# Rebuilding the state-space stage of a fused two-block kernel: scale folded into the regrouping, spins by pairs, read-out by quarters

## The chip, the cores and the metric

The kernel runs on one core of a Trainium2 chip. The metric is the device time of one execution in microseconds (us), lower is better. The core's engines are TensorE (PE in the rows; PEld is its weight load), VectorE (DVE), ScalarE (ACT), GpSimd (POOL) and SyncE (SP), which here only issues DMAs. Every matmul, transpose, vector and scalar operation is written by hand in the order in which its engine executes it, and semaphores tie the engines together.

## What is computed

Two blocks of a model with 256 tokens and width 1024, one after the other, all in fp32: pooling mixer, stick-breaking attention, two softmax attentions, an MLP, a state-space mixer (S5) with a gated linear unit, and another MLP. The change is in the S5 mixer:

```python
def s5_mixer(h, ...):                       # h = rms_norm(x) * gain, 256 x 1024
    u = h.reshape(S, 64 groups, 16)
    bu = einsum('gpi,lgi->lgp', b_bar, u)   # complex, 64 states per group
    hs = scan(h_t = a_bar * h_{t-1} + bu_t) # along the 256 tokens
    y = einsum('gop,lgp->lgo', c, hs).real + d_skip * u
    g = gelu(y)
    val, gate = split(g @ w_glu, 2)
    return val * sigmoid(gate)
```

## The kernel before

**The S5 stage.** The 256 tokens are taken as 32 steps of L = 8 tokens. Inside a step the recurrence is a fixed 128 x 128 matrix per group, the taps; between the steps runs a scan of 32 elements per state. In order:

1. The last products of the first MLP fill four banks (`acc`). VectorE adds each to `x` (line 2151), and for each of the four there is a pair of DMAs, one from SP (line 602) and one from ScalarE (line 1494), that copies `x` into `xch`, with a step's eight tokens side by side. Beside that ScalarE squares `x` (1496), GpSimd makes the root (2218), and VectorE spreads the row scale over a table (`rrow`, 2164). TensorE turns this table into `rmap` (1085), the scale of every step and token.
2. VectorE waits for all eight copies and regroups `xch` into `xg` in four plain copies (2169). TensorE turns `xg` in four units of four transposes (1092), and VectorE empties each turn into `ug` while it multiplies by `rmap` (2177).
3. TensorE makes the drive of the states in four banks, `inject` 0 to 3, of 32 small matmuls each (1105), then the tap product in four banks of 16 matmuls (1117). Its weights are read from a scratch tensor in DRAM by 16 DMAs of SP, `toep_in` (568): part 0, eight of them, before the copies of `x`, part 1, the other eight, after them. They land in the slots of split weights (`whi`, `wlo`) that the weights `val` 0 need next.
4. VectorE runs `spin(n)`, n = 0 to 3, one for each inject bank: it turns the drive by cosines and sines (1667, 1668, 1670, 1671), scans (1674, twice), turns back (1677, 1678) and writes `states` (1682, twice). Most steps wait for the one before them.
5. TensorE adds the states to the tap product, the read-out (1133): banks 0 and 1 (part 0) after spin 1, banks 2 and 3 (part 1) after spin 3. Half 0 of the groups is in banks 0 and 2, half 1 in banks 1 and 3.
6. ScalarE empties the four banks into `yc` (1504), TensorE turns `yc` (1142), ScalarE applies Gelu (1509) and makes the high part `hT_hi` (1514), VectorE the low part (2188), and TensorE begins the product `val` 0 (688 to 690).

**What sets the order of the rest.** A weight is split into a high part by ScalarE (1220, 128x2048, "fill") and a low part by VectorE (1585) for fp32 accuracy from three fast matmuls. The fills of `val` 0, halves 0 and 1, stand on ScalarE ahead of the four emptyings of item 6, and on VectorE behind spin 3. The rows of `val` 0 come by two DMAs of SP (608) that wait for inject 3. SP has one queue, in this order: taps part 0, copies of `x`, taps part 1, read-out weights of part 1 (642), `val` 0, then ring loads.

```python
b = filled(("inject", n))[:, :].rearrange("p (m r c) -> p r m c", m=2, r=2)
link(dve.tensor_tensor(spun, b, both[0], ALU.mult))          # link: wait for its end
dve.tensor_tensor(crossed, b[:, ::-1], both[1], ALU.mult)
for r in range(2):
    ins = dve.tensor_tensor_scan(faded[:, r], fade, driven[:, r], 0.0, ALU.mult, ALU.add)
```

## Time and profile before

| | |
|---|---|
| time, median of 3 runs | 887.88 us (885.32 to 888.23) |
| the profiled execution, its own time | 886.7 us |
| its span in the trace | 884.9 us |
| granted TensorE clock, mean over the span | 0.986 of full speed |
| TensorE busy | 857.9 us, 97% of the span |
| VectorE busy | 592.9 us, 67% |
| ScalarE busy | 440.4 us, 50% |
| DMA, mean | 176 GB/s |

### The profile page before, as it was taken

The numbers are of one execution on the slowest core, as the hardware profiler recorded it, in microseconds if no ns is written. First come the engines' busy times: TensorE is split into PE (matmuls) and PEld (weight loads), VectorE is DVE, ScalarE is ACT, GpSimd is POOL, SyncE is SP. The second block draws the span as 40 slices with busy tenths as digits, with TensorE's granted clock in tenths as the row PEclk, the third lists the DMA queues.
The fourth block names the chain that finished last, engine by engine and source line by source line (L and its number), as shares of the span: only waits on it lengthen the run. The fifth ranks groups of instructions, "written<-read, shape, count | busy, mean of one in ns | idle before, by whom it ended". The sixth has DMA issues, their size and how long they took to land.

```text
span 884.9 us, 13373 instructions
## 1 busy us (share of the span) xinstructions
PE 857.9 (97%) x5611; PEld 744.5 (84%) x5611; DVE 592.9 (67%) x746; ACT 440.4 (50%) x585; POOL 113.1 (13%) x74
## 2 busy tenths in 40 slices
PE   6999999999999999999999999996989999999998
PEld 5886888888788878888999888885978899999996
DVE  4694577766756769787878888773875665555553
ACT  5644465656954656644534436442074544444441
POOL 1000001111000023131333334430000000000000
PEclk9999999999999999999999999998599999999999
DMA  8936645555014438126466556647766555555521
GB/s 294 341 127 232 240 146 191 190 190 182 10 40 149 140 96 285 49 96 214 144 222 202 175 196 217 216 167 156 256 221 207 174 190 191 190 190 190 190 96 48
DMA packets 67253, 155.96 MB, mean 176 GB/s; under 512 B 3017, under 2 KB 6826, under 8 KB 66938
## 3 DMA queue, kind: packets, MB, share of 16 engines
q1 hardware_dynamic: 63888, 146.28, 49.2%
q0 software_dynamic: 2224, 7.67, 2.6%
q10 hardware_dynamic: 1082, 1.16, 0.7%
q8 instruction: 45, 0.74, 0.3%
q14 instruction: 14, 0.11, 0.0%
HBM read 146.70 MB, written 7.34 MB: 174 GB/s over the span
## 4 chain that ended last, share of the span: by engine, by line
PE 88%; DVE 8%; ACT 2%; DMA 1%; issue 1%; ACTq 0%; DVEq 0%
PE bank L688 18%; PE bank L689 18%; PE bank L690 18%; PE bank L1000 7%; PE bank L1002 7%; PE bank L998 7%; PE bank L681 2%; PE bank L783 2%; PE bank L773 1%; DMA work<-x 1%; PE bank L1063 1%; PE bank L884 1%; DVE aux L1674 1%; DMA cst<-in_tables 1%; PE bank L823 1%
## 5 line engine op out<-in xcount | busy, mean ns | idle before, releaser
L1585 DVE TENSOR_TENSOR wlo<-ring,whi 128x2048 fp32r<-128x2048 f32 (+1 forms) x104 | 253.7, 2443 | 139.6 <-ACT whi L1220 139.3
L1220 ACT ACTIVATE whi<-ring 128x2048 fp32r<-128x2048 f32 (+1 forms) x105 | 200.5, 1909 | 214.8 <-PE bank L690 148.3
L688 PE MATMUL bank<-whi,hT 128*128 128x512 f32 (+1 forms) x512 | 201.8, 394 | 4.3 <-DVE hT L2188 2.3
L690 PE MATMUL bank<-whi,hT 128*128 128x512 f32 (+1 forms) x512 | 199.5, 390 | 0.0
L689 PE MATMUL bank<-wlo,hT 128*128 128x512 f32 (+1 forms) x512 | 199.4, 389 | 0.0
L998 PE MATMUL bank<-hT,whi 128*128 128x256 f32 x512 | 145.4, 284 | 0.0
L1000 PE MATMUL bank<-hT,whi 128*128 128x256 f32 x512 | 144.8, 283 | 0.0
L1002 PE MATMUL bank<-hT,wlo 128*128 128x256 f32 x512 | 144.8, 283 | 0.0
L688 PEld LDWEIGHTS bank<-whi,hT 128*128 128x128 f32 x512 | 96.7, 189 | 25.3 <-issue 4.4
L690 PEld LDWEIGHTS bank<-whi,hT 128*128 128x128 f32 x512 | 96.5, 189 | 19.6
L689 PEld LDWEIGHTS bank<-wlo,hT 128*128 128x128 f32 x512 | 96.7, 189 | 19.0 <-issue 0.2
L998 PEld LDWEIGHTS bank<-hT,whi 128*128 128x128 f32 x512 | 98.1, 192 | 0.6
L1000 PEld LDWEIGHTS bank<-hT,whi 128*128 128x128 f32 x512 | 98.2, 192 | 0.5
L1002 PEld LDWEIGHTS bank<-hT,wlo 128*128 128x128 f32 x512 | 98.1, 192 | 0.0
L688 PE MATMUL bank<-whi,hidT_hi 128*128 128x512 f32 x224 | 88.2, 394 | 0.0
L689 PE MATMUL bank<-wlo,hidT_hi 128*128 128x512 f32 x224 | 87.5, 390 | 0.0
L690 PE MATMUL bank<-whi,hidT_lo 128*128 128x512 f32 x224 | 87.2, 389 | 0.0
L1580 DVE SCALAR_TENSOR_TENSOR wlo<-ring,vcols,whi 128x512 fp32r<-128x512 f32 x64 | 43.8, 747 | 20.5 <-ACT whi L1216 20.5
L1216 ACT ACTIVATE whi<-ring,vcols 128x512 fp32r<-128x512 f32 x64 | 40.9, 711 | 19.2 <-PE bank L690 17.0
L688 PEld LDWEIGHTS bank<-whi,hidT_hi 128*128 128x128 f32 x224 | 42.1, 188 | 9.9 <-issue 1.4
L690 PEld LDWEIGHTS bank<-whi,hidT_lo 128*128 128x128 f32 x224 | 42.1, 188 | 8.9
L689 PEld LDWEIGHTS bank<-wlo,hidT_hi 128*128 128x128 f32 x224 | 42.1, 188 | 8.3
(278 smaller groups left out, 1026.9 us busy)
## 6 DMA issues: line engine op xcount, KB each, us to landing
ring<-in_w_ff SPq DMA_DIRECT2D x64, 1024.0 KB, 5.3
ring<-in_ple_gate_w SPq DMA_DIRECT2D x8, 1024.0 KB, 5.1
ring<-in_w_kv SPq DMA_DIRECT2D x8, 1024.0 KB, 5.0
ring<-in_b_w_in SPq DMA_DIRECT2D x8, 1024.0 KB, 5.0
ring<-in_a_w_in SPq DMA_DIRECT2D x7, 1024.0 KB, 13.0
ring<-in_w_in SPq DMA_DIRECT2D x6, 1024.0 KB, 5.3
ring<-in_w_glu SPq DMA_DIRECT2D x6, 1024.0 KB, 6.6
ring<-in_a_w_out SPq DMA_DIRECT2D x4, 1024.0 KB, 5.8
```

Of the source, the lines that this page charges most:

```text
L681: last = pe.transpose(b[0:width, cc * S + t * P:cc * S + t * P + P], src[:, t, c * width:(c + 1) * width], ident)
L688: pe.matmul(bank_cols, high[:, at[0], at[1]], w_high, start=first, stop=False)
L689: pe.matmul(bank_cols, high[:, at[0], at[1]], w_low, start=False, stop=False)
L690: return pe.matmul(bank_cols, low[:, at[0], at[1]], w_high, start=False, stop=last)
L783: last = pe.matmul(b[:, :], pT[:, l, k, t * P:(t + 1) * P], ple_rows[:, k, nb * 512:(nb + 1) * 512], start=(k == 0), stop=(k == 1))
L998: pe.matmul(b[:, at:at + S], w_high[:, kk, cols], hT_hi[:, k, :], start=k == 0 and at == 0, stop=False, skip_group_check=True)
L1000: pe.matmul(b[:, at:at + S], w_high[:, kk, cols], hT_lo[:, k, :], start=False, stop=False, skip_group_check=True)
L1002: last = pe.matmul(b[:, at:at + S], w_low[:, kk, cols], hT_hi[:, k, :], start=False, stop=k == KC - 1, skip_group_check=True)
L1216: ins = act.activation(whi[at][:, n], ring[:, slot[name], cols][:, n], ACT.Copy, scale=gain(gained[name[0]], 4 * (g % 2) + kk))
L1220: act.activation(whi[at], raw_rows(g), ACT.Copy).then_inc(high_made, 1)
L1580: ins = dve.scalar_tensor_tensor(out=wlo[at][:, n], in0=ring[:, slot[name], cols][:, n], scalar=gain(gained[name[0]], 4 * (g % 2) + kk), i ...
L1585: dve.tensor_tensor(wlo[at], raw_rows(g), whi[at], ALU.subtract).then_inc(low_made, 1)
```

## The change

- **Scale.** The table is smaller (`row_of`, 8 columns), `rmap` comes from two accumulated matmuls with the constant `chunk_of`, and VectorE copies it before it waits for the copies of `x`. The four regrouping instructions become multiplications by `rmap`. `xg` lies in another place (over `hT`).
- **Turns.** ScalarE, not VectorE, empties the four turns into `ug`, by plain copies.
- **Taps.** SP issues only the first four of the eight DMAs of part 0 before the copies of `x`, the other four after them, ahead of part 1.
- **Spins.** `spin_pair` takes two inject banks: sums, scans and (for pair 0) the turning back work on both. Pair 1 turns back in two halves and signals after each.
- **Order on TensorE.** Taps part 0, read-out part 0, taps part 1, read-out part 1. The tap product goes through the four output quarters in its inner loop. Read-out part 1 is split in two by quarters of the output, each for both halves of the groups.
- **Emptying.** VectorE empties bank 2, ScalarE banks 0, 1 and 3. ScalarE's fill of `val` 0 half 0 stands between bank 1 and bank 3, its fill of half 1 behind the first two Gelus, and VectorE's low parts are moved to match.
- **Constant matmuls.** `constant_products` puts 14, 4, 8 and 8 fp32 matmuls on a constant into idle banks; nothing reads them.

```diff
+KEEP = (14, 4, 8, 8)
...
     for b in range(4):
-        u.add(("ug", b), "v")
+        u.add(("ug", b), "a")
...
+            u.add(("state_out", n), "v" if n == 2 else "a", bank=n)
...
                 if name == ("readout", 1):
-                    toep_in(0)
+                    toep_in(0, (0,))
...
                     sp.wait_ge(x_chunked, 16 * 8)
+                    toep_in(0, (1,))
                     toep_in(1)
...
+            def constant_products(name, count):
+                idle = begin(name)
+                for _ in range(count):
+                    pe.matmul(idle[:, 0:P], allneg[:, :], allneg[:, :], start=True, stop=True, skip_group_check=True)
+            constant_products(("ug", 0), KEEP[0])
             b = begin(("rmap", 0))
...
+            constant_products(("ug", 0), KEEP[1])
...
-                for q in range(4):
-                    for s in range(4):
+                for s in range(4):
+                    for q in range(4):
                         last = pe.matmul(b[32 * q:32 * q + 32, s * P:(s + 1) * P]...,
...
+            for part in range(2):
+                pe.wait_ge(toep_landed[part], 16 * 8)
+                for half in range(GH):
+                    tap_product(2 * part + half)
+                constant_products(("state_outT", 0), KEEP[2 + part])
+                weights_here(("readout", part))
+                if part == 0:
+                    pe.wait_ge(states_ready, 1)
+                    for half in range(GH):
+                        read_out(0, (half,), range(4))
+                else:
+                    pe.wait_ge(states_ready, 2)
+                    read_out(1, (0, 1), (0, 1))
+                    pe.wait_ge(states_ready, 3)
+                    read_out(1, (0, 1), (2, 3))
...
-            refill(("f2", 0, FB - 2), 1)
-            refill(("f2", 0, FB - 1), 0)
             for n in range(4):
+                b = filled(("ug", n))
+                act.activation(to, b[:, :]..., ACT.Copy).then_inc(act_emptied, 1)
+            for n in (0, 1, 3):
+                if n == 3:
+                    refill(("f2", 0, FB - 2), 1)
                 b = filled(("state_out", n))
...
+            def spin_pair(pair):
+                for odd in range(2):
+                    b = filled(("inject", 2 * pair + odd))...
+                    dve.tensor_tensor(spun[:, :, m], b, both[0][:, :, m], ALU.mult)
+                    dve.tensor_tensor(crossed[:, :, m], b[:, ::-1], both[1][:, :, m], ALU.mult).then_inc(dve_emptied, 1)
...
+                for m in (slice(0, 2), slice(2, 4)) if pair else (slice(0, 4),):
+                    dve.tensor_tensor(spun[:, :, m], faded[:, :, m], both[0][:, :, m], ALU.mult)
+                    link(dve.tensor_tensor(crossed[:, :, m], faded[:, ::-1, m], both[1][:, :, m], ALU.mult))
...
+            b = filled(("rmap", 0))
+            dve.tensor_copy(rmap, b[:, 0:L]).then_inc(dve_emptied, 1)
             dve.wait_ge(x_chunked, 16 * 8)
             for n in range(4):
-                dve.tensor_copy(xg[:, l:l + 4], xch...).then_inc(regrouped, 1)
+                dve.tensor_tensor(xg[:, l:l + 4], xch..., rmap..., ALU.mult).then_inc(regrouped, 1)
```

VectorE from the waiting for the copies of `x` to the first spin. Before (2169 regroups, 2172 copies `rmap`, 2177 empties the turns, from 1667 on the first spin):

```order
L2169 COPY aux<-work 128x512 [waits x_chunked]
L2169 COPY aux<-work 128x512 x3
L2172 COPY aux<-bank 128x32 [waits pe_done]
L2177 TENSOR_TENSOR work<-bank,aux 128x4x4x32 [waits pe_done,dve_emptied]
L2177 TENSOR_TENSOR work<-bank,aux 128x4x4x32 [waits pe_done] x3
L1667 TENSOR_TENSOR aux<-bank,h 128x512 [waits pe_done,fades_ready,waves_ready]
```

And now, with the whole of pair 0:

```order
L2212 COPY aux<-bank 128x8 [waits pe_done]
L2217 TENSOR_TENSOR xg_at<-work,aux 128x512 [waits x_chunked,dve_emptied]
L2217 TENSOR_TENSOR xg_at<-work,aux 128x512 x3
L1710 TENSOR_TENSOR aux<-bank,h 128x2x256 [waits pe_done,fades_ready,waves_ready]
L1711 TENSOR_TENSOR aux<-bank,h 128x2x256
L1710 TENSOR_TENSOR aux<-bank,h 128x2x256 [waits pe_done]
L1711 TENSOR_TENSOR aux<-bank,h 128x2x256
L1713 TENSOR_TENSOR aux<-aux 128x512 [waits dve_emptied]
L1714 TENSOR_TENSOR aux<-aux 128x512
L1717 SCALAR_TENSOR_TENSOR pT<-sig,aux 128x512 [waits dve_step]
...
L1721 TENSOR_TENSOR aux<-pT,h 128x1024 [waits dve_step]
...
L1727 TENSOR_TENSOR aux<-aux 128x4x4x31 [waits dve_step]
```

The copy of `rmap` moved ahead of the wait for the copies of `x`, the emptying of the turns left VectorE, and in pair 0 two instructions stand where four stood for sums and turning back (1717, 1721 and 1727 each come with a second one of the same shape).

SP around the copies of `x`, before (568 taps, 602 copies, 642 read-out weights, 608 `val` 0):

```order
L568 DMA spare<-scratch_taps 128x1x512 x7
L602 DMA work<-x 16x8x256 [waits dve_emptied,pe_done]
L602 DMA work<-x 16x8x256 [waits dve_emptied] x3
L568 DMA spare<-scratch_taps 128x1x512 [waits taps_stored0,zeros_stored,taps_stored1,first_used,x_chunked]
...
L642 DMA ring<-scratch_readout 128x4096 [waits readout_stored1,readout_stored0,low_made]
L608 DMA work<-in_w_glu 128x4x512 [waits pe_done]
```

And now (573, 607, 648 and 614 are the same four):

```order
L573 DMA spare<-scratch_taps 128x1x512 x3
L607 DMA work<-x 16x8x256 [waits dve_emptied,pe_done]
L607 DMA work<-x 16x8x256 [waits dve_emptied] x3
L573 DMA spare<-scratch_taps 128x1x512 [waits taps_stored0,zeros_stored,taps_stored1,f2_done,x_chunked]
...
L573 DMA spare<-scratch_taps 128x1x512 [waits taps_stored0,taps_stored1,zeros_stored,first_used]
...
L648 DMA ring<-scratch_readout 128x4096 [waits readout_stored1,readout_stored0,low_made]
L614 DMA work<-in_w_glu 128x4x512 [waits pe_done]
```

Four transfers of 256 KB went from ahead of the copies to behind them, so that twelve, not eight, stand between the copies and the read-out weights.

## Rows read from the trace of the kernel before

**Rows 1.** The profile's chain that ended last: share of each engine
```profile
PE 88%; DVE 8%; ACT 2%; DMA 1%; issue 1%; ACTq 0%; DVEq 0%
```
**Rows 2.** Busy by stretch: stretch, us, PE, PEld, DVE, ACT, POOL busy, PEclk, DMA share, GB/s
```profile
610.30:614.10 3.80, 0.00 (x1) 0.00 (x0) 1.20 (x5) 2.35 (x3) 0.72 (x1) 1.00 1.05 121
614.10:618.60 4.50, 1.01 (x5) 0.94 (x5) 0.85 (x4) 0.08 (x1) 0.00 (x0) 0.50 0.23 28
618.60:622.20 3.60, 3.60 (x16) 3.27 (x16) 3.51 (x7) 0.00 (x0) 0.00 (x0) 0.50 0.81 214
622.20:636.00 13.80, 13.80 (x257) 13.74 (x256) 10.37 (x19) 0.00 (x0) 0.00 (x0) 0.50 0.77 251
636.00:644.90 8.90, 8.90 (x133) 8.40 (x132) 8.56 (x17) 1.91 (x1) 0.00 (x0) 0.89 0.67 238
...
652.00:656.10 4.10, 1.83 (x16) 1.60 (x17) 1.91 (x3) 4.07 (x6) 0.00 (x0) 1.00 1.05 396
656.10:667.00 10.90, 10.87 (x48) 9.03 (x49) 6.36 (x5) 6.61 (x6) 0.00 (x0) 1.00 0.67 236
```
**Rows 3.** The chain of waits, 590 to 700 us: start, us, what
```profile
611.12 6.80 DMA work<-x
...
622.27 3.58 PE bank L1105 x64
...
648.62 3.35 PE bank L1133 x128
```
**Rows 4.** Timeline, 596 to 700 us: start, us, engine, line, operation; spin 3
```profile
642.95 0.69 DVE L1667 TENSOR_TENSOR aux<-bank,h 128x512 f32<-128x512 f32 x1
643.68 0.69 DVE L1668 TENSOR_TENSOR aux<-bank,h 128x512 f32<-128x512 f32 x1
644.40 0.42 DVE L1670 TENSOR_TENSOR aux<-aux 128x256 f32<-128x256 f32 x1
644.74 0.42 DVE L1671 TENSOR_TENSOR aux<-aux 128x256 f32<-128x256 f32 x1
...
645.19 1.27 DVE L1674 TENSOR_TENSOR_SCAN aux<-sig,aux 128x256 f32<-128x256 f32 x2
646.50 0.69 DVE L1677 TENSOR_TENSOR aux<-aux,h 128x512 f32<-128x512 f32 x1
...
647.11 0.68 DVE L1678 TENSOR_TENSOR aux<-aux,h 128x512 f32<-128x512 f32 x1
647.83 0.74 DVE L1682 TENSOR_TENSOR aux<-aux 128x248 f32<-128x248 f32 x2
```
**Rows 5.** The same timeline, from the last read-out to the product `val` 0
```profile
651.87 1.97 PE L1142 MATMUL bank<-cst,work 128*128 128x128 f32 x16
652.00 0.60 ACT L1504 ACTIVATE work<-bank 128x512 f32<-128x512 f32 x1 [0.76 <-PE bank L1133]
652.56 2.03 ACT L1509 ACTIVATE work<-bank 128x512 f32<-128x512 f32 x2
654.62 1.15 ACT L1514 ACTIVATE hT<-work 128x512 fp32r<-128x512 f32 x2
655.29 1.29 DVE L2188 TENSOR_TENSOR hT<-work,hT 128x512 fp32r<-128x512 f32 x2 [2.19 <-ACT hT L1514]
```
**Rows 6.** DMA issues, 595 to 665 us: queue, count, KB each, median us to landing
```profile
spare<-scratch_taps SPq DMA_DIRECT2D x16, 256.0 KB, 5.1
ring<-scratch_readout SPq DMA_DIRECT2D x1, 2048.0 KB, 11.5
...
work<-x ACTq DMA_DIRECT2D x4, 128.0 KB, 7.0
```
**Rows 7.** Instructions of line 1769: count, duration ns min/median/max
```profile
L1769 DVE TENSOR_TENSOR work<-pa,bb x8: 1211/1213/1219, 432.6 to 594.9; 128x1024 f32<-128x1024 f32 x8
```
**Rows 8.** Groups by line and form, TensorE: count, busy us, mean ns
```profile
L836 PE MATMUL bank<-aux,allneg 128*128 128x128 f32 x32 | 6.5, 286 | 0.0
```
**Rows 9.** The page's groups by line: count, busy us, mean ns, idle before
```profile
L1220 ACT ACTIVATE whi<-ring 128x2048 fp32r<-128x2048 f32 (+1 forms) x105 | 200.5, 1909 | 214.8 <-PE bank L690 148.3
```

More of the change, by code:

```diff
@@ L77, in constants @@
     put("skip_at", i[:, None] % 32 == i[None, :])
[L78 removed]
+    put("row_of", i[:, None] % L == L - 1 - i[None, 0:L])
     put("ramp", np.arange(NC)[None, :])
[L80 removed]
+    put("chunk_of", np.concatenate([(i[None, :] // 16 % NT == t) & (i[:, None] // L == i[None, :] % 16)
+                                    for t in range(NT)], axis=1))
     put("mask_st", np.where(i[:, None] >= i[None, :], BIG, 0))
@@ L222, in plan @@
     for b in range(4):
-        u.add(("ug", b), "v")
+        u.add(("ug", b), "a")
     for b in range(4):
         u.add(("inject", b), "v")
-    for n in range(4):
-        u.add(("toep", n), "", bank=n)
-    for n in range(4):
-        u.add(("state_out", n), "a", bank=n)
+    for part in range(2):
+        for n in (2 * part, 2 * part + 1):
+            u.add(("toep", n), "", bank=n)
+        for n in (2 * part, 2 * part + 1):
+            u.add(("state_out", n), "v" if n == 2 else "a", bank=n)
     for b in range(4):
@@ L555, in _, with toep_in @@
         def _(sp):
-            def toep_in(part):
+            def toep_in(part, pairs=(0, 1)):
                 if part == 0:
@@ L563, in toep_in @@
                     sp.wait_ge(taps_stored[b], 16 * (part + 1))
-                for pair in range(2):
+                for pair in pairs:
                     for s in range(4):
@@ L1084, in _ @@
             for t in range(NT):
-                last = pe.matmul(b[:, 16 * t:16 * t + 16], const("same_j"), rrow[:, t, :], start=True, stop=True)
+                at = slice(P * t, P * t + P)
+                last = pe.matmul(b[:, 0:L], const("chunk_of")[:, at], rrow[:, t, :], start=t == 0, stop=t == NT - 1)
             last.then_inc(pe_done, 1)
+            constant_products(("ug", 0), KEEP[1])
             for n in range(4):
@@ L1120, in _, with read_out @@
                 last.then_inc(pe_done, 1)
-            for n in range(4):
-                b = bank(("state_out", n))
-                part, half = n // 2, n % 2
-                pe.wait_ge(states_ready, 2 * part + 2)
-                rows = slice(GP * half, GP * half + GP)
-                weights_here(("readout", part))
+            def read_out(part, halves, quarters):
                 wr = weights(("readout", part), 32, P)
@@ L1130, in _, with state_turn @@
                     for r in range(2):
-                        for q in range(4):
-                            m = 4 * part + q
-                            last = pe.matmul(b[32 * q:32 * q + 32, s * P:(s + 1) * P],
-                                             states[rows, 8 * m + 4 * r + s, :], wr[rows, 8 * q + 4 * r + s, :],
-                                             start=False, stop=(r == 1), skip_group_check=True)
-                last.then_inc(pe_done, 1)
-            for n in range(4):
+                        for half in halves:
+                            rows = slice(GP * half, GP * half + GP)
+                            for q in quarters:
+                                last = pe.matmul(bank(("state_out", 2 * part + half))[32 * q:32 * q + 32, s * P:(s + 1) * P],
+                                                 states[rows, 8 * (4 * part + q) + 4 * r + s, :], wr[rows, 8 * q + 4 * r + s, :],
+                                                 start=False, stop=(r == 1), skip_group_check=True)
+                            if s == 3 and r == 1 and q == 3:
+                                last.then_inc(pe_done, 1)
+            def state_turn(n):
                 b = begin(("state_outT", n))
                 half = n // 2
-                emptied(("state_out", 2 + half))
+                for part in range(2):
+                    emptied(("state_out", 2 * part + half))
                 for jj in range(4):
@@ L1143, in _ @@
                 last.then_inc(pe_done, 1)
+            for part in range(2):
+                pe.wait_ge(toep_landed[part], 16 * 8)
[12 more added lines that the diff above has]
+                    read_out(1, (0, 1), (2, 3))
+            for n in range(4):
+                state_turn(n)
             for hh in range(2):
@@ L1676, in spin @@
                 link(ins)
[L1677 to L1684 removed]
+                for m in (slice(0, 2), slice(2, 4)) if pair else (slice(0, 4),):
+                    dve.tensor_tensor(spun[:, :, m], faded[:, :, m], both[0][:, :, m], ALU.mult)
+                    link(dve.tensor_tensor(crossed[:, :, m], faded[:, ::-1, m], both[1][:, :, m], ALU.mult))
+                    for r, op in enumerate((ALU.subtract, ALU.add)):
+                        one, two = (v[:, r, m].rearrange("p m (q c) -> p m q c", c=NC)[:, :, :, 0:NC - 1]
+                                    for v in (spun, crossed))
+                        to = states[:, 32 * pair:32 * pair + 32, :].rearrange("p (m r q) c -> p r m q c", m=4, r=2)[:, r, m, :, 1:NC]
+                        ins = dve.tensor_tensor(to, one, two, op)
+                    ins.then_inc(states_ready, 1)
+                    dve.wait_ge(states_ready, (2 if m.start == 0 else 3) if pair else 1)
             def s5_powers():
```

75 lines of the change are left out of this document (33 added, 42 removed).

## The prediction

> **What bounds the kernel now.** I read the chain of the whole execution first: 88% of it is TensorE [rows 1]. So an edit counts only where TensorE waits, or runs slowly while something waits for it. The busy time by stretch shows where [rows 2]: from 610.3 to 656.1 us TensorE is either empty or full of short instructions, and from 656.1 on it is full again (10.87 of 10.90 us) and stays so. I call the start of the product `val` 0, at 656.1, the point P. What comes after P is bound by TensorE and unchanged, so the gain is the time by which P comes earlier.
>
> The chain of waits between the two ends has five links:
> - the last copy of `x`, 6.8 us from 611.1 to 617.9 [rows 3];
> - regrouping and turns, 617.95 to 622.2 = 4.25 us;
> - inject 0 up to spin 0, 3.8 us, of which 3.58 are its matmuls [rows 3];
> - four spins on VectorE, 626.0 to 648.6 = 22.6 us. The steps of one spin [rows 4] begin 0.73, 0.72, 0.34, 0.45, 1.31 (both scans), 0.61 and 0.72 us apart, and the last takes 0.78 up to the next: 5.66 us;
> - the tail, 648.6 to 656.1 = 7.5 us: read-out of two banks 3.35 [rows 3], then 4.1 for emptying, turn, Gelu, high part, low part [rows 5].
>
> The reader should see in rows 2 that the granted clock is 0.50 (1.2 GHz) from 614.1 to 636.0. It fell after TensorE had run nothing from 610.3 to 614.1 (0.00 us busy).
>
> **The change, link by link.**
>
> *Copies of `x`: 1.5 us gained.* Four transfers of 256 KB leave the stretch ahead of the copies, in which the DMA share is full (1.05 in the last piece, [rows 2]). Issue to landing was 7.0 us in the median on ScalarE's queue, and 6.8 for the last. The taps, twice as large per transfer, land in 5.1 us [rows 6]. I put the last copy between these, nearer to the taps because its queue should now be empty: 5.3 us, at 616.4. Bounds: nothing gained (6.8), or 2.3 us (4.5, somewhat under the taps' median, the copies being half as large). The copy of `rmap` must now be done by then; its table is ready at 614.4, and 1 us later it is. It costs nothing under the copies.
>
> *Regrouping and turns: 1.2 us.* Four plain copies become four multiplications of 128x512, which begin 0.61 us apart (line 1677 to 1678, [rows 4]): the last ends at 618.9. A turn of four transposes is 0.9 us at 1.2 GHz (3.6 us for 16, [rows 2]) and 0.5 us at 2.4 GHz (1.97 for 16, [rows 5]), so inject 0 begins at 619.4: 3.0 us instead of 4.25. The turns are emptied by ScalarE, 0.60 us each [rows 5]; it is idle there, and the first inject needs only the second turn. If ScalarE were not idle, the third would still be hidden by inject 0.
>
> *Inject 0: 1.8 us,* all from the clock. At 1.2 GHz 128 matmuls took 13.8 us [rows 2]; at 2.4 GHz I take half, 1.75 us for 32 with 0.25 for handing over. No row shows this shape at 2.4 GHz; the bounds are half and no gain at all. I take half, because transposes halved (3.6 to 1.97). Spin 0 begins at 621.4.
>
> The clock is what the constants are for. A transpose is one record and a fp32 matmul two, so one constant costs about 2 x 1.97/16 = 0.25 us; the row of the same form gives at most 6.5/16 = 0.41 [rows 8]. Fourteen last 3.5 us, from 610.3 to 613.8, just before the table (614.4); at 0.41 they would end at 616.0 and still be hidden by the copies. Four more fill 614.9 to 615.9. The longest idle stretch left is 1.5 us, against the 3.8 that preceded the fall.
>
> *Spins: 1.7 us.* Pair 0: four products of 512, 3 x 0.61 + 0.72 = 2.55; a wait of 0.5 for inject 1, which ends 1.75 us after inject 0 while VectorE is ready after 1.2; sums 0.61 + 0.72 = 1.33; two scans of 512, less than twice 1.31: 2.4; two products of 1024 at 1.2 [rows 7], 2.35; two writes 1.3: together 10.4. Pair 1: 2.55 + 1.33 + 2.4 and twice (0.61 + 0.72 + 0.78): 10.5. Together 20.9 instead of 22.6. Bounds: scans of 2.2 to 2.7 us, so 1.1 to 2.1 gained. The second half of pair 1 is signalled at 621.4 + 20.9 = 642.3, the first at 640.2.
>
> *Tail: 0.85 us.* After the last signal half of a part's read-out is left, 3.35/2 = 1.7 us. Banks 2 and 3 are emptied side by side (0.7), which the first turn (0.5) then waits for; in the old order that turn was hidden behind an emptying. From the first Gelu to P it is 656.1 - 652.6 = 3.5 [rows 5]. With 0.2 for handing over 6.65 instead of 7.5. P is at 649.0.
>
> *What rests on cover.* Tap product, 16 constants and read-out part 0 run under the spins. Injects end at 626.5. In rows 2 the 64 matmuls of the tap product took 8.9 us at a mean clock of 0.89, so at most 4 us a part; taps 0 ends at 630.5, constants 632.5, read-out 0 (spin pair 0 ready at 631.8) 635.9, taps 1 639.9, constants 641.9, then the two quarters-pairs of 1.7: 645.3 instead of 644.0. So with taps as slow as now TensorE is late by 1.3 us. But four consecutive matmuls now write different quarters, as the read-out does, whose 64 matmuls take 3.35 us [rows 3], 1.7 a part; I take this, and nothing is late. The Trainium skill says the same ("TensorE: Matmul & The Clock Gate", section "Part 3: Packing small matmuls — row/col tiling"): matmuls whose outputs lie in different groups of 32 partitions run side by side. By it the sum stands at 7.0; by the row of the tap product it would be 5.7.
>
> The fill of `val` 0 half 0 (1.9 us on ScalarE, [rows 9]) now stands ahead of the emptying of bank 3, so it must start by 642.0. Its rows come behind 3.15 MB of taps and 2.1 MB of read-out weights, 6.3 MB with its own half. At 251 GB/s, the mean of the stretch that held such transfers [rows 2], that is 25 us from 616.4: 641.5. At rest these queues reach 396 GB/s, so it should be nearer 639. I cost it at nothing, with a cover of 0.5 to 3 us. The fill of half 1 (1.9 us) delays the later Gelus; their channels are needed 5.5 us after P (half of the 10.9 for this product, [rows 2]), at 654.5, and are ready about then (649.0 - 0.8 + 1.9 + 2.15 + 1.3 = 653.6).
>
> **The sum.** 1.5 + 1.2 + 1.8 + 1.7 + 0.85 = 7.05 us. Against the profiled execution that is 886.7 - 7.05 = 879.65. The median of the runs is 1.2 above it and gives 887.88 - 7.05 = 880.8. I take the middle, 880.2.
>
> **The rivals.**
>
> *The clock falls all the same.* Then inject 0 takes 3.8, pair 0 waits for inject 1 (3.45 us after inject 0, so 2.2 instead of 0.5), turns end 0.45 later: last signal 642.3 + 0.45 + 1.8 + 1.7 = 646.2. But TensorE is then the later one: injects end 619.9 + 13.8 = 633.7, taps 0 4.0, constants 2.0, read-out 3.35, taps 1 and constants 3.7, read-out 3.35, so 650.1, and P 650.1 + 4.9 = 655.0. A gain of 1.1: 886.2. For it: 13.8 us of injects and 3.6 us of transposes did not lift the clock [rows 2], so perhaps neither holds it. Against it: from 652.0 to 656.1 TensorE ran 1.83 us of transposes and nothing else, and the clock stayed 1.00. The same page of the Trainium skill, "Part 4: PE-mode transpose", states that a transpose does not count as busy in the way a matmul does; by it the stretch from the last constant to inject 0, 615.9 to 619.4, would be 3.5 us of rest, near the 3.8 that was followed by a fall. The turns at 0.50 agree with it, the last stretch does not. Chance 0.15.
>
> *The quarters do not run side by side, or the copies land no earlier.* 5.7 or 5.55 us gained, 881.5 to 882. Within the forecast's own range; chance 0.15. Both together: 883.
>
> *Slower: the weights of `val` 0 come late.* ScalarE waits for them with bank 3, the last turn's source, queued behind. Every us after 642.0 costs one. The gain is gone when the first half lands at 649, that is when 6.3 MB move at under 194 GB/s. At 175 GB/s they land at 652.4, the forecast's P moves by 10.4, and the time is 890.6. For it: the stretches with small transfers had 121 and 214 GB/s [rows 2]. Against it: those held the copies of `x`, or began before the taps flowed; the stretch with taps and read-out weights had 251. Chance 0.06.
>
> **How the numbers follow.** Forecast 0.64, its variants 0.15, clock 0.15, late weights 0.06. A difference of 0.3% (2.7 us, about what a measurement of this kernel can tell from no change) puts the border of faster at 885.2. Forecast and variants lie below it (0.79), of the clock case a fifth (0.03). No change: the rest of the clock case and mild lateness, 0.12. Slower: 0.06. The forecast's own range is 877.5 (copies 0.8 better, scans 0.4, weaker waits) to 883; to hold 8 in 10 with the clock case half in it the range is 877.5 to 886.0.
>
> **What would show it.** Clock 1.00 from 610 through the injects; first regrouping at about 616.4 and not 617.9; inject group 1.75 us, not 3.45; two pairs in 20.9 us; 64 matmuls of taps in 3.5 us; ScalarE's fill of `val` 0 over before bank 3 is full; P at about 649. Wrong it is if the clock drops between 611 and 625, if ScalarE waits for a DMA in front of bank 3, or if TensorE runs constants while a signalled state waits.

## The result, and the profile after

| | median (range), runs | ratio to before, 95% interval |
|---|---|---|
| before | 885.55 us (882.86 to 888.23), 20 | |
| the change | 887.52 us (885.15 to 891.64), 20 | 1.0025 [1.0016, 1.0035] |

The change is 2.0 us slower, where the forecast had 7 us faster. The profiled execution of the change took 885.15 us, the fastest of its twenty; its span is 883.3 us, its mean granted clock 0.996. P is at 654.58 us, not at 649.0. From P to the start of the last matmul, which is what "to the end" means from here on, both kernels take 224.52 us. So the stretch up to P decides, as the prediction assumed.

The busy time by stretch of the change, with the columns of [rows 2]. The stretches are: early constants after the last sum of the MLP, turns, injects, the rest of the spins, taps 1 to read-out 1, tail.

```profile
609.90:613.70 3.80, 3.10 (x28) 2.91 (x27) 1.23 (x5) 2.38 (x3) 0.73 (x1) 1.00 0.56 90
...
616.10:619.80 3.70, 3.67 (x18) 2.78 (x18) 2.84 (x3) 1.79 (x3) 0.00 (x0) 0.55 0.96 249
619.80:630.30 10.50, 8.02 (x257) 7.91 (x256) 7.75 (x10) 0.60 (x1) 0.00 (x0) 0.97 1.08 284
630.30:642.90 12.60, 10.02 (x240) 8.72 (x242) 12.28 (x19) 1.19 (x3) 0.00 (x0) 0.89 0.72 278
642.90:649.40 6.50, 6.48 (x192) 5.89 (x181) 0.00 (x0) 1.81 (x2) 0.00 (x0) 1.00 0.89 305
649.40:654.60 5.20, 1.96 (x17) 1.79 (x17) 3.75 (x4) 4.17 (x6) 0.00 (x0) 1.00 0.79 263
```

The clock did most of what was wanted: it was 1.00 or near it but for two dips to 0.50, of 3.4 us each, from 616.0 (the turns) and from 629.6. The first is one of the forecast's signs of being wrong ("if the clock drops between 611 and 625"), but it cost little: from the start of the regrouping to inject 0 it is 4.72 us, against 4.52 in the second look below, where the clock was 1.00. But in the row of the injects TensorE is busy for 8.02 us of 10.50 with nothing to wait for, and from 642.90 on VectorE stands still (0.00) while TensorE works for 6.5 us. The chain of waits gives both causes; its columns are start, us, what.

```profile
610.70 4.25 DMA work<-x
...
619.83 5.71 PE bank L1120 x190
625.55 2.48 issue
628.02 2.54 PE bank L1120 x66
630.57 3.10 PE bank L1132 x61
633.67 1.20 issue
634.87 0.41 PE bank L1132 x3
635.28 1.98 PE bank L1092 x16
637.26 2.79 PE bank L1145 x109
640.05 1.38 issue
641.43 0.84 PE bank L1145 x19
642.27 1.88 PE bank L1132 x64
644.16 1.98 PE bank L1092 x16
646.14 3.31 PE bank L1145 x128
```

(1120 injects, 1132 taps, 1092 constants, 1145 read-out.) From inject 0 to the end of the read-out the chain never leaves TensorE; in [rows 3] the read-out of the last banks stood behind the spins. And three times, for 5.06 us in all, TensorE stops for nothing that this chain shows. The timeline of the change says how early the states were ready:

```profile
621.97 0.69 DVE L1710 TENSOR_TENSOR aux<-bank,h 128x512 f32<-128x512 f32 x1 [3.02 <-PE bank L1120]
...
642.11 0.75 DVE L1727 TENSOR_TENSOR aux<-aux 128x248 f32<-128x248 f32 x2
...
642.80 1.90 ACT L1254 ACTIVATE whi<-work 128x2048 fp32r<-128x2048 f32 x1
...
649.49 0.69 DVE L2225 COPY work<-bank 128x512 f32<-128x512 f32 x1 [6.63 <-PE bank L1145]
```

Two pairs of spins take 621.97 to 642.86 = 20.9 us, as forecast, and then VectorE waits 6.63 us for the read-out. The gain of the spins exists and reaches nobody. The fill of `val` 0 (line 1254) starts without waiting for a DMA.

### The profile page after: what moved, and what is told of

It is laid out like the page before. It is cut to its first block, busy times and chain, and to the rows that moved or that the text cites. A ratio compares the mean times of both kernels' runs of the same rounds, so it can differ in the third digit from the quotient of the medians.

```text
span 883.3 us, 13493 instructions
## 1 busy us (share of the span) xinstructions
PE 856.6 (97%) x5679; PEld 741.8 (84%) x5679; DVE 590.8 (67%) x731; ACT 442.1 (50%) x588; POOL 113.0 (13%) x74
## 4 chain that ended last, share of the span: by engine, by line
PE 87%; DVE 5%; DMA 3%; ACT 2%; issue 1%; SPq 1%; ACTq 0%; DVEq 0%
PE bank L694 18%; PE bank L696 17%; PE bank L695 17%; PE bank L1008 7%; PE bank L1006 7%; PE bank L1004 7%; PE bank L687 2%; DMA ring<-in_a_w_in 2%; PE bank L789 2%; PE bank L1120 1%; DMA x<-in_x 1%; PE bank L1145 1%; PE bank L779 1%; DVE wlo L1625 1%; PE bank L1069 1%
```

## What the kernel before does in another execution

The prediction rested on one execution of before (886.7 us, 1.1 above the median now known). **A second look at before**, unchanged:

> The kernel before, unchanged, for a second profile. Its runs have mean granted clocks of 0.986 to 0.994, and the profile that the prediction used had 0.986. Theory: that profile showed one of the rarer executions, with 23.9 us at half clock; in most the clock comes back after one piece of a few us, and the injects run at full clock already. Then this profile, if its clock is about 0.993, shows injects in 7 to 10 us instead of 13.8 and the product val 0 begins some 2 to 4 us earlier after the last sum. If its clock is 0.986 again it says nothing new.

Measured: 883.7 us. The injects and the tail in its busy time by stretch, then TensorE's rows of its timeline:

```profile
620.10:631.20 11.10, 9.22 (x257) 9.11 (x256) 8.56 (x16) 0.00 (x0) 0.00 (x0) 0.81 0.93 309
...
649.00:653.20 4.20, 1.90 (x17) 1.69 (x17) 2.00 (x3) 4.13 (x6) 0.00 (x0) 1.00 1.05 390
```
```profile
620.07 7.59 PE L1105 MATMUL bank<-work 128*64 128x32 f32 x226
629.53 1.91 PE L1105 MATMUL bank<-work 128*64 128x32 f32 x30 [1.88 <-issue]
631.37 9.90 PE L1117 MATMUL bank<-spare,work 128*32 128x128 f32 x128
...
645.66 3.31 PE L1133 MATMUL bank<-ring,aux 64*32 64x128 f32 x128 [1.14 <-DVE aux L1682]
```

Three things differ from [rows 2 to 5]. The copies of `x` land after 4.84 us, not 6.80. The clock is higher through the injects (0.81, not 0.50), low only for 6.8 us from 614.9 and again from 628.6; inject 0, which begins at 620.07 where the change has 619.76, costs 2.8 us and not 3.58. And TensorE waits only 1.14 us for the last states: it was nearly the later engine in before already. P is at 653.17, 1.4 us ahead of P in the fastest execution of the change.

How often each kind occurs can be read from the mean clock of every execution. The four sets of runs measured beside the experiments hold 113 executions of before: 41 have a mean clock of 0.988 or less, with a median of 886.9 us, and 61 have 0.992 or more, with a median of 884.2. So the profile behind the forecast (0.986) stands for about one execution in three, and the second one (0.992, 883.7 us) is a slightly fast one of the larger group.

The copies of `x` can be compared over more profiles too. With all eight taps ahead of them they landed after 6.80, 4.84, 5.77, 5.92 and 6.40 us, in five profiles; with four ahead, after 4.25 to 4.33 us, in the eleven whose chain passes through them.

**A second look at the change**, unchanged:

> The change, unchanged, for a second profile: its first, 885.2 us, was the fastest of its 20 runs. Expected in a typical one of 887.5 us: a fall of the clock just behind the start of val 0 with 226.1 us from there to the end, instead of 224.5, and stops of TensorE with no releaser that add up to 5 us or more before it.

Measured: 887.54 us, P at 656.97. Chain of waits:

```profile
620.70 5.71 PE bank L1120 x190
626.42 2.76 issue
629.18 3.76 PE bank L1120 x66
632.94 3.13 PE bank L1132 x64
636.07 1.98 PE bank L1092 x16
638.05 2.79 PE bank L1145 x109
640.84 1.38 issue
642.22 1.49 PE bank L1145 x18
643.71 2.83 PE bank L1132 x64
646.54 1.98 PE bank L1092 x16
648.52 3.31 PE bank L1145 x128
```

Two of the three stops and both groups of constants are there again; the stops add up to 4.14 us, under the 5 that I expected. Taps 1 now took 2.83 us, against 1.88 in the first profile, with the clock at 0.50 for 3.4 us from 642.2. The fall of the clock behind P that I expected is not in this profile: from P to the end it took 224.51 us.

## What the stops are

The chains of all kernels show where TensorE stops. In the change it is after 190 records of the injects, then 66 + 61 = 127, then 3 + 16 + 109 = 128 records later. (A record here is one matmul record; each has a weight load, so 128 records are 256 instructions; single records can be missing from the trace.) **Wide constants** test whether the count decides. The edit makes 5 constants of 512 columns out of the 18 early ones of 128, leaves the late ones out, and puts 3 wide ones ahead of `val` 0, where the kernel of comparison (884.74, below) has 10 narrow ones:

```diff
-KEEP = (14, 4, 8, 8)
+KEEP = (4, 1, 0, 0)
-                    pe.matmul(idle[:, 0:P], allneg[:, :], allneg[:, :], start=True, ...)
+                    pe.matmul(idle[:, :], allneg[:, :], cst[:, 0:512], start=True, ...)
...
+            constant_products((("gate", 0), 0, 0), 3)      # ahead of val 0
```

> As the last, with constants of 512 moving columns, a quarter as many (4, 1, and 3 at the end): the same TensorE time from 40 instead of 112 instructions. TensorE ran out of instructions three times in the profile of the change; 72 fewer of 256 per block shifts or shortens the first stall. If supply is what limits, the first stall (3.4 us without late constants) shrinks by 1 us or more or moves out of the injects and the time falls by up to 1 us against f2; if only the position of the block boundary counts, it moves and the time stays within 0.5 us.

Measured: 885.71 us (884.79 to 888.97), 1.0011 [0.9996, 1.0025], no better than with narrow ones (885.81 without any ahead of `val` 0, 884.74 with ten). The expectation counted the instructions wrongly: the 8 wide constants are 32 of them, not 40, and ahead of the injects the edit saves 52. Its chain:

```profile
619.94 6.42 PE bank L1120 x216
626.36 3.10 issue
629.46 2.14 PE bank L1120 x40
631.60 2.65 PE bank L1132 x64
634.25 0.78 PE bank L1145 x23
635.03 1.09 issue
```

Thirteen fewer constants are 26 fewer records, and the stop moved from the 190th to the 216th record of the injects; the next one comes 40 + 64 + 23 = 127 later. So a stop belongs to a place in the instruction stream, every 256 instructions, and not to a buffer or to data. The page has a DMA queue of that kind:

```profile
q8 instruction: 45, 0.74, 0.3%
```

45 transfers of 16 KB, and the program has 2 x 5679 TensorE instructions, 44.4 times 256. I take it that TensorE's instructions come by these transfers, and that it stops when the next has not landed. The counts match, and the single packets of this queue, whose times the traces hold, bear it out. In the first profile of the change three of them start at 625.34, 632.38 and 639.06 and land at 626.55, 633.40 and 640.16; TensorE goes on at 628.02, 634.87 and 641.43, 1.3 to 1.5 us behind each landing. The packet before these started at 604.35, and TensorE began 546 instructions between the two starts, where the mean is 256: the transfer had fallen behind. The 18 profiles of this case hold 32 stops of 0.28 us or more, between the table and the tail, for which the trace has no semaphore to wait for, and every one ends 1.0 to 1.7 us behind a landing in this queue.

The Trainium skill ("Runtime: NRT & Kernel Launch", section "Instruction fetch mechanics") states the same blocks of 16 KiB or 256 instructions, with the cost mostly hidden. The first half agrees with these counts, the second does not hold in this stage: at full clock 256 instructions of injects are used in 3.9 us, and from one resumption to the next it takes 6.85 and 6.56 us (628.02, 634.87, 641.43).

If the stream of instructions shares the DMA engines with the taps, it should help to hold the taps back. **All late taps after the injects:**

```diff
                     toep_in(0, (1,))
+                    sp.wait_ge(pe_done, done(("inject", 3)))
                     toep_in(1)
```

> The change, but SP waits for inject 3 before it issues taps part 1 (and with it the read-out weights), so that between the landing of taps part 0 and the end of the injects the DMA engines carry nothing but TensorE's own instructions. If the stall of 2.5 us in the injects comes from the DMA load, it falls below 1 us here and the instruction transfer starts or lands earlier. If it is inherent in the rate of short matmuls at full clock, it stays at 2 us or more. The time itself may rise by some us, since these weights then land late.

Measured: 886.53 us (885.03 to 888.08), 1.0020 [1.0006, 1.0035]. Its chain:

```profile
620.60 3.88 PE bank L1121 x128
...
633.32 3.38 PE bank L1146 x109
636.70 3.23 issue
639.92 1.49 PE bank L1146 x19
```

No stop in the injects: they are over at 628.1, 7.6 us after their start, where the change needs 10.7 and 12.3 in its two profiles. The stop came back in read-out 0, once the transfers flowed again, so the time barely moved. The DMA engines were 0.12 busy during these injects, and 1.08 during those of the change up to the stop.

The other profiles sort in the same way. Ten have their injects wholly or mostly at full clock beside the taps, and each has a stop in them, of 1.7 to 3.5 us. Six have taps part 1 held back, and none has one. Two have the injects at half clock (the first one of before, and the one without constants below), and none has one there.

**Behind the stops the clock falls.** In each of the ten the granted clock fell to 0.50 between 1 and 4 us after the stop in the injects began (625.55 and 629.6 in the change). In the six without such a stop it was 1.00 throughout the injects and to 633.6 or later, and fell then in or behind a wait or a later stop of TensorE. That the stop brings the fall is read from this order of events; no run changes one without the other. What the low clock costs is seen behind the stop: the last 66 records of the injects and taps 0 take 2.54 + 3.10 + 0.41 = 6.05 us in the first profile of the change and 6.89 in the second. At full clock, by the 3.88 us for 128 records above and the 1.88 of taps 1, they would take 3.9.

## Parts of the change, one at a time

**Without the late constants.**

```diff
-KEEP = (14, 4, 8, 8)
+KEEP = (14, 4, 0, 0)
```

> The change with the two late groups of constant matmuls gone (KEEP 14, 4, 0, 0). In the profile of the change TensorE, not VectorE, ends the stage: between the last instruction of the spins (642.9 us) and the last read-out (649.4) it does taps part 1 (1.9), eight constants (2.05) and read-out (3.3). Theory A, the constants sit on the path: both groups cost about 2.0 us each there, so the time falls by 3 to 4 us. Theory B, TensorE waits for its own instructions and the stream is only shifted: the stalls stay or move, and the time falls by 1 us or less. Theory C, the late constants hold the clock: without them it falls again and the time rises by 1 to 3 us.

Measured: 885.81 us (884.71 to 887.0), 1.0010 [0.9996, 1.0024]: 1.7 us below the change by the medians, 1.3 by the ratios. The constants occupied 2 x 2 us of TensorE, and some of that came back in longer stops (3.20 and 2.66 us) and in a longer low clock (6.8 us from 627.8). P moved to 653.88, but the granted clock fell to 0.70 in the stretch behind it:

```profile
653.90:656.90 3.00, 3.00 (x10) 2.40 (x11) 1.97 (x2) 3.00 (x3) 0.00 (x0) 0.70 0.69 260
```

From P to the end it took 226.15 us, not 224.5. **Ten constants directly ahead of `val` 0,** after the turns and with nothing behind them to delay, on top of that kernel:

```diff
+            constant_products((("gate", 0), 0, 0), 10)
```

> The change without its two late groups of constants, but with ten constants behind the last turns, in TensorE's wait for the high and low parts. In four of five profiles the clock fell within 1 us after the product val 0 had begun and stayed at half for 3.4 us, and from that product's start to the end took 226.1 us instead of 224.5. If the wait before the product is the reason, the fall goes and with it 1.6 us: 1.6 us faster than the run without late constants, about 884.2. If the constants delay the product instead (they take 2.2 us in a wait of 2.6), it is no faster.

Measured: 884.74 us (883.28 to 886.41), 1.0000 [0.9989, 1.0011], and 224.52 us from P to the end. By the profiles the fall cost 1.6 us, and it is in none of the six profiles of kernels with these ten constants; by the times the step of 1.1 us lies within the intervals of both. That the constants prevent the fall is therefore possible and not shown. I build on this version.

**Without any constants.**

```diff
-KEEP = (14, 4, 8, 8)
+KEEP = (0, 0, 0, 0)
```

> The change with no constant matmuls at all. If the early 18 hold the clock through turns and injects, this is 2 us or more slower than the run without the late groups, with injects at 0.50 clock (13.8 us). If their use is small because the clock falls in most executions anyway, both are within 1 us. By the theory that TensorE lacks instructions: at 0.50 clock a block of instructions lasts longer and the stalls of 2.5, 1.2 and 1.4 us without a releaser shrink to nothing.

Measured: 887.93 us (886.25 to 889.34), 1.0038 [1.0024, 1.0052]. In its profile the clock is low through the injects and the first taps:

```profile
616.20:636.70 20.50, 19.51 (x308) 18.34 (x312) 13.46 (x16) 2.39 (x4) 0.00 (x0) 0.50 0.91 259
```

As expected there is no stop in the injects at half clock; one of 2.88 us stands later, in taps 1 (from 641.97). Against the version without the late ones alone, the early constants are worth 2.1 us; against the change as a whole, with its late ones, all constants together are worth nothing that shows.

**The early constants in before.**

```diff
+            constant_products(("ug", 0), 14)               # ahead of the table
             b = begin(("rmap", 0))
...
+            constant_products(("ug", 0), 8)                # behind it
```

> The kernel before with 14 constants before the table of scales and 8 behind it, and nothing else of the change. Theory A (as I forecast): the clock stays up, injects take 7 us instead of 13.8, the first spin begins 2.7 us earlier, and the time falls by about 2.5 us. Theory B (instruction supply): the clock stays up and TensorE then stops for 1 to 3 us per 256 instructions, but the spins hide that, since only inject 0 is on their path: a gain of 1 to 2.5 us. Theory C: in most executions of before the clock is back early anyway: within 0.5 us of before.

Measured: 885.52 us (881.73 to 888.99), 1.0008 [0.9990, 1.0025]. In the profile the clock stayed 1.00 up to the injects (621.6), a bank of which took 2.07 us instead of 3.58. Eleven of the twelve executions have a mean clock of 0.990 or more, so the constants did hold it up, and yet the time did not move; its interval has room for a gain of 0.9 us and for a loss of 2.2. That most executions of before have the clock back by then anyway explains a part; the rest stays open.

**The taps of part 0 back ahead of the copies of `x`.**

```diff
-                    toep_in(0, (0,))
+                    toep_in(0)
...
-                    toep_in(0, (1,))
```

> The change with all eight taps transfers of part 0 ahead of the copies of x again. The copies landed at 615.0 in the profile of the change (4.25 us after the last residual sum) against 6.8 before. If that gain is real it goes: regrouping begins 2 to 2.5 us later, and the time rises by that (about 2 us), less if TensorE's stalls shrink because 1 MB less is under way during the injects (then 0 to 1 us).

Measured: 887.85 us (886.54 to 889.17), 1.0038 [1.0024, 1.0051]. Its chain:

```profile
611.71 6.40 DMA work<-x
...
623.24 5.76 PE bank L1119 x190
629.00 3.01 issue
...
643.01 0.28 issue
```

The copies take 2.1 us longer than with the change (4.25), and inject 0 begins at 623.17. But P is at 656.43, no later than in the second look at the change: the last stop shrank from 1.38 to 0.28 us. In these profiles most of a head start at inject 0 is eaten by the stops.

**Single spins,** the four of before in place of the two pairs, without late constants (the diff puts back the function `spin` and its signals 1 to 4):

```diff
-            def spin_pair(pair):
+            def spin(n):
...
-                    pe.wait_ge(states_ready, 1)
+                    pe.wait_ge(states_ready, 2)
```

> The change without late constants (885.8 us), with the four single spins of before in place of the two pairs. The pairs save 1.7 us on VectorE. If TensorE is the late one in most executions, taking them back costs under 0.5 us; if VectorE still ends the chain, it costs 1.2 to 1.9 us.

Measured: 885.86 us (884.53 to 886.38), 0.9996 [0.9984, 1.0007], beside 885.81 with pairs, which were measured in another set of runs; by the ratios to before of each set the single spins are 1.2 us faster, within the intervals. Either way the 1.7 us of the pairs are worth nothing while TensorE is late.

## Towards a version that beats both

All of these stand on the kernel with ten constants ahead of `val` 0. **Taps spaced:**

```diff
                     toep_in(0, (1,))
+                    sp.wait_ge(pe_done, done(("inject", 1)))
                     toep_in(1)
```

> The run with ten constants before val 0 and none late (884.7 us), and SP waiting for inject 1 before taps part 1. In seven profiles TensorE stopped with no releaser for 1.2 to 3.7 us about every 6.2 to 6.9 us, after 256 instructions, and did not stop in the injects where the DMA engines were quiet. Theory supply: its instructions arrive by DMA behind bulk data; a quiet stretch around inject 1 removes the first stop (3.7 us), and the product val 0 begins 1 to 2 us earlier, unless the read-out weights become late. Rival, the stop depends on where the block ends only: it stays, and the time stays within 0.5 us.

Measured: 884.29 us, 0.9981 [0.9968, 0.9994]. (Two of its twelve executions, of 2155 and 3007 us, are disturbed and not in the ratio; without them the median is 884.16.) By the ratios that is 1.7 us below the version it stands on. No stop in the injects, small ones later.

**Read-out 1 bank by bank** instead of by quarters, so that bank 2 is emptied and turned while bank 3 is computed:

```diff
-                    pe.wait_ge(states_ready, 2)
-                    read_out(1, (0, 1), (0, 1))
                     pe.wait_ge(states_ready, 3)
-                    read_out(1, (0, 1), (2, 3))
+                    for half in range(GH):
+                        read_out(1, (half,), range(4))
```

> The same base (884.7 us), with read-out part 1 bank after bank, as before, instead of by quarters over both banks. From the end of the last read-out to the product val 0 took 5.5 us in the change and 4.2 in the kernel before. If TensorE, not VectorE, ends the chain, splitting by quarters bought nothing and its tail costs 1.2 us: this run is 1.0 to 1.3 us faster, about 883.6. If VectorE ends the chain in typical executions, it is 0.5 us or more slower.

Measured: 884.50 us (882.16 to 888.3), 0.9988 [0.9971, 1.0004]; not told apart from 884.74.

**Both:**

> Both edits. If each works alone and they add, 882.5 us or so, which would be 0.2% under the kernel before (884.6).

Measured: **882.98 us** (882.49 to 885.35), 0.9968 [0.9957, 0.9979]. It beats before by 2.5 us in the same set of runs, 2.8 by the ratio, and the change by 4.5. Its one profile was the slowest of the twelve (885.35), and has a stop of 3.14 us at 636.15 and the clock at 0.50 for 13.7 us from 638.5, so I don't read P from it.

**Both, with single spins:**

> The fastest version so far (spaced taps, read-out by banks, 883.0 us) with the four single spins of before. Taking the pairs back cost nothing in the change without late constants (885.9 against 885.8). If TensorE is still the late one here, it costs under 0.5 us again; if the looser supply gave the lead back to VectorE, it costs 1.0 to 1.7 us.

Measured: 883.96 us (883.16 to 888.3), 0.9989 [0.9974, 1.0005]. Now the pairs are worth 1.0 us by the medians, 1.9 by the ratios, though the two intervals overlap a little. In its profile VectorE ends the stage again: the read-out begins at 645.04, directly behind the last states.

**Both, without early constants:**

```diff
-KEEP = (14, 4, 0, 0)
+KEEP = (0, 0, 0, 0)
```

> The fastest version so far (883.0 us) without its early 18 constants, its last ten kept. If they hold the clock through turns and injects and this helps, 1 us or more slower (in the change itself all constants away cost 2.1 us against only the late ones away). If the second profile of before is typical, in which the clock came back for the injects without any constant, within 0.5 us.

Measured: 888.53 us (886.13 to 892.62), 1.0034 [1.0017, 1.0052], 5.5 us slower. Its busy time by stretch from taps 0 to P:

```profile
634.00:656.00 22.00, 21.03 (x343) 19.14 (x336) 13.72 (x20) 8.47 (x9) 0.00 (x0) 0.54 0.95 354
```

The clock is low from 634 on, 20 us behind the place of the constants. All twelve executions have a mean clock of 0.976 to 0.987, against 0.991 to 0.996 with the constants, which fits a gain by the clock. As the one profile of the kernel with them has a low stretch there too, though a shorter one, the runs do not show by which stretch.

**The spacing in before:**

```diff
                     toep_in(0)
...
+                    sp.wait_ge(pe_done, done(("inject", 1)))
                     toep_in(1)
```

> The kernel before, with SP waiting for inject 1 before taps part 1, and nothing else. If supply of instructions matters there too, its stop in the injects (1.9 us in its second profile) goes; but VectorE ends its chain, so the time stays within 0.5 us, or rises by 1 to 4 us in executions in which the injects run at half clock and the taps therefore arrive after they are wanted.

Measured: 887.56 us (886.59 to 889.11), 1.0027 [1.0013, 1.0040], a loss. Its timeline:

```profile
638.45 6.99 PE L1118 MATMUL bank<-spare,work 128*32 128x128 f32 x64 [5.67 <-DMA spare<-scratch_taps]
```

In before all taps come ahead of read-out 0, so held-back taps stop TensorE for 5.67 us. The spacing pays only with the new order, in which read-out 0 stands between the two halves of the taps.

## Why the prediction was wrong

**The step that failed is "What rests on cover".** It let TensorE's work run under the spins with nothing late, and costed the late constants at nothing. Measured in the first profile, the read-out ended at 649.45, not 644.0. Of these 5.45 us, 0.56 are VectorE's (last states at 642.86, not 642.3). The other 4.9 are TensorE's. It stopped for 5.06 us in the injects, the taps and read-out 0, because its own instructions had not come. I had no term for that. The profile that I read has no such stop; the second one of before has one, of 1.88 us. Beside the stops, the injects took 8.25 us and not 7.1, and taps 0 took 3.51 and not 1.75, at the clock that fell behind the first stop. Against all this the forecast had 1.6 us of slack before read-out 0 (626.5 + 1.75 + 2.0 = 630.25 against 631.8); it began at 637.26. So what I had placed in cover came onto the path: nearly all of taps 1 (1.88), the constants (1.98) and the whole of read-out 1 (3.31) run behind the last state instead of half a read-out. My last sentence named this sign ("if TensorE runs constants while a signalled state waits"), and it is what the profile shows, at 644.16.

**The base.** The median of three runs that I started from, 887.88, is 2.3 us above that of the twenty, and the links were read from an execution of a kind that is one in three. Its low clock lasted from 614.1 to past the injects without a break; in the second profile it lasted 6.8 us twice. *Inject 0: 1.8 us* was therefore there to gain in a part of the executions only, and the early constants in before changed nothing that shows. *Copies of `x`: 1.5 us* was right in cause and size: the five profiles with all taps ahead have 5.9 us in the mean, the eleven others 4.3. Against the second profile of before it is only 0.5.

**Regrouping and turns: 1.2 us.** The four multiplications took 3.9 us (x4, in the second look), 0.97 us apart and not 0.61. The row of line 1677 had the same shape, but another layout of its operands. The plain copies of before read the same source in the same order, and all four took 2.14 us, so the source alone is not the reason; what is was not tried. From the start of the regrouping to inject 0 it is 4.7 us, where I had 3.0 and before has 4.3: 0.5 lost and not 1.2 gained. The turns were emptied by ScalarE without delay.

**Spins: 1.7 us.** Right to 0.1 us: 20.9 us, with the wait of 0.48 for inject 1. Off the path as long as TensorE is late.

**Quarters side by side.** Right: the 32 matmuls (64 records) of taps 1 take 1.88 us at a clock of 1.00, where I had 1.75, against 9.90 for all 64 in the second look at before, 4 us of it at half clock.

**Tail: 0.85 us gained.** It lost 1.0. From the end of the read-out to P I had 4.95 us against 4.15 of before, paid for by half a read-out that runs ahead of the last signal. Measured are 5.13 against 4.16, and with TensorE late no half ran ahead. Read-out by banks, with the taps spaced, is 1.2 us better (884.16 to 882.98).

**The rivals.** The clock case described P at 655.0 and TensorE as the later engine, with 886.2 us. Its P is close to that of the first profile (654.58), but by luck: the clock was 0.97 in the injects, and the time is 1.3 us over what it gave. The late weights of `val` 0 did not come about: the fill began at 642.80, behind bank 1, with no wait. The reason given for a fall, that the turns are rest for TensorE, is not borne out: in ten of the twelve profiles of versions of the change with early constants the clock stayed at 1.00 from them into the injects. No rival had TensorE's own instructions as the bound.

**Where the 7 us went,** first profile of the change against the second of before, each counted from the last sum of the MLP (start of its last matmul, 609.49 and 609.74). At the start of spin 0 the change is 0.8 us ahead, where the forecast had 4.5. Against the first profile of before it would be 3.6: the forecast's gain up to there exists in the slower third of the executions. At the last state it is 2.55 ahead, thanks to the pairs. At the end of the read-out it is 0.7 behind: TensorE's stops, the constants and taps 1 took 3.2 us. The tail takes 1.0 more, so P is 1.7 later. Shown by runs of their own are the price of the late constants, the pairs' gain going nowhere, and the tail (in company with the spacing). How the rest divides between the stops and the clock that falls behind them was not separated.

## What to carry to other kernels

Before work is costed as "under cover", add up the covering engine's time at the speed at which it will run, with what it may lack for itself: an engine with 1 us of slack is no cover. Read the mean clock and the time of the profiled execution against the other runs, and take a second profile where a term rests on a clock that happened to be low. Where "issue" stands in the middle of one line's group in the chain, look for a transfer of instructions that landed just before the engine went on. Filler matmuls belong where nothing is behind them: the late ones here cost 1.3 to 1.7 us and gave nothing that shows. Fewer and wider ones did not help.

## What the runs showed of the hardware

- TensorE can stop at every 256th instruction (128 matmul records with their loads), for 0.3 to 3.5 us, when it runs short matmuls at full clock beside full DMA engines: in ten of ten profiles with such injects, and in none of the six in which the taps were held back and 256 records took 7.6 us. Each stop ends 1.0 to 1.7 us behind the landing of a transfer of 16 KB in the queue "instruction". This is why a faster order, a higher clock or an earlier start brought less than it gained.
- In those ten profiles the granted clock fell to 0.50 within 1 to 4 us of the start of the stop, and in the two profiles of the change stops of 2.5 and 2.8 us were followed by short matmuls that took 2.2 and 3.0 us more than at full clock.
- The same kernel has its low clock at different places: through the whole of the injects in one execution of before, for 6.8 us twice in another. And the early constants, worth nothing that shows in before, are worth 5.5 us in the best version.
- The clock can fall behind P, at 1.6 us of loss: four of the eleven profiles of kernels with only turns in the tail show it (226.10 to 226.15 us from P to the end), none of the six with ten constants there (224.50 to 224.55). With four in eleven, none in six would come about by chance once in seven times, and all four are from the first set of experiments, so it is not shown that the constants prevent it. They take 2.23 us of TensorE where it would be idle.
